# Expert 0's rows picked by one-hot matmuls from tiles kept on chip, index matmuls and overflow tables moved into the experts

## The chip, the cores and the metric

The kernel runs on one core of one Trainium2 chip. The metric is the device time of one execution in microseconds, as the median of several runs. The engines are TensorE (PE; its weight loads are listed as PEld), VectorE (DVE), ScalarE (ACT), GpSimd (POOL) and SyncE (SP), and transfers run on 16 DMA engines.

## The reference, cut to what matters

```python
SEQ = 512; D_MODEL = 1024; DEPTH = 2; N_EXPERTS = 16; N_GROUPS = 4; TOP_K = 2; D_EXPERT = 512

for l in range(DEPTH):
    sh1, sc1, g1, sh2, sc2, g2 = jnp.split(silu(c) @ w_ada[l] + b_ada[l], 6, axis=-1)
    h = modulate(rmsnorm(x, norm1_g[l]), sh1, sc1)
    x = x + g1 * mixer(h, ...)                  # retention, pooling, projections
    h = modulate(rmsnorm(x, norm2_g[l]), sh2, sc2)
    x = x + g2 * moe(h, ...)                    # the part that the change touches
return rmsnorm(x, final_g)

def moe(h, ...):
    probs = softmax(h @ w_router + b_router)    # 512 tokens x 16 experts
    # the group (of 4) with the largest sum of its two best, and in it the two best experts
    expert_idx, weights = route(h, ...)
    # every expert works on the tokens that chose it
    y_e = (silu(x_e @ w_gate[e]) * (x_e @ w_up[e])) @ w_down[e]
    # each token gets the weighted sum of its two experts' rows
```

All arrays are float32.

## The kernel before, in words

The program is written out by hand for each engine: every engine has its own function in which its instructions stand in order, and semaphores order the engines among each other (`wait_ge` waits, `then_inc` counts up). No planner moves anything. There are two layers, and each has a mixer of 17 groups of matmuls and then the experts.

*Weights.* All weights come as pieces of 512 KB through a ring of eight `raw` slots, which SyncE fills as `raw_used` counts up. In the expert stage eight more pieces per layer lie in `ahead`. Products are made at float32 accuracy from two parts: ScalarE writes the high part of a piece, `w_hi`, VectorE the rest, `w_lo = raw - w_hi`, both in rings of four slots, and TensorE makes three passes (`three_passes`, L1389 to L1392). An expert has 12 pieces (0 to 3 and 4 to 7 for gate and up, 8 to 11 for down), and each is six matmuls of 512 columns. `lo_e(n)` and `hi_e(n)` are numbered so that 12 to 15 in expert e are pieces 0 to 3 of expert e + 1; piece n needs the ring slot of piece n - 4 to be used.

*Second norm.* `norm_tile(l, 1, "h2", t)` normalises the four token tiles of 128 rows into `h_nat`, a buffer with two slots. From t = 2 on it waits for the transposes of tile t - 2 and for that tile's store to DRAM (`row_stored`). GpSimd stores each tile twice into `h_rows`. TensorE transposes the tiles for the router.

*Routing.* On VectorE `route_tokens` makes one-hot rows of both choices of each token (`hots`), whose sum is `chosen`. TensorE counts from it each token's place within its expert and each expert's total (`pos_ready`). VectorE copies the places into `pos`, picks each token's own into `posk` (`both_chosen`), and makes eight one-hot matrices `hot` (token against slot). TensorE multiplies them with the token numbers `hotid`; that gives for every expert the row number in each of its 128 slots, and VectorE converts these to `idx` and, with empty slots set to row 0, to `idx_any`. GpSimd then gathers the rows of experts 0 to 3 from `h_rows` into `xg0` to `xg3` with four indirect DMAs. TensorE transposes expert 0's rows (`gathered_transposes`), ScalarE and VectorE split them into `xgT_hi` and `xgT_lo`, and expert 0 starts. In between TensorE runs dummy matmuls of 512 columns (`keep_busy(n)`): 29 ahead of the counts, 11 behind them, 28 behind the index matmuls.

*Overflow.* An expert has 128 slots. If one had more tokens, extra blocks would run after expert 15. The tables for that are made in any case: the first part at the end of `route_tokens` (L1159 to L1188), the second in `overflow_slots` (L1190), which VectorE runs behind expert 0's `gathered_lo`, ahead of expert 0. Their results are read first at expert 15 (`slots_ready`).

*Expert stage.* In order on VectorE, `expert(l, e)` is: `lo_e(4)`, `lo_e(5)`, first half of the last expert's `y_out`, `hidden(0)`, `lo_e(6)`, second half of `y_out`, `lo_e(7)`, `hidT(0)`, `lo_e(8)`, `lo_e(9)`, `hidden(1)`, `lo_e(10)`, `hidT(1)`, `lo_e(11)`, `lo_e(12)`, the next expert's `gathered_lo` in two halves around `lo_e(13)`, `lo_e(14)`, `lo_e(15)`. TensorE runs pieces 0 to 5, the transposes of the hidden rows' first half, pieces 6 to 9 (the second half's transposes within piece 9), the next expert's `gathered_transposes`, and pieces 10 and 11. For each expert GpSimd gathers the rows of expert e + 4 and scatters `y_out` of expert e to `y_rows`.

Of the kernel before, what the change touches and what calls it, by code (L numbers as in the profile page):

```python
# [17 lines left out]
F32 = mybir.dt.float32  # L18
F32R = mybir.dt.float32r
I32 = mybir.dt.int32  # L20
# [4 lines left out]
P = 128  # L25
# [154 lines left out]
def build(nc, w, x_in, c_in, consts, rotary, ada_rows, pool_w, pool_scale, final_g, out):  # L180
# [7 lines left out]
    with ExitStack() as ctx:  # L188
# [11 lines left out]
        def sb(name, shape, dtype, offset):  # L200
            return nc.alloc_sbuf_tensor_at(name, shape, dtype, offset=offset)
# [52 lines left out]
        y_sq = sb("y_sq", [P, DV], F32, Dr + 10240)  # L254
        h_nat = sb("h_nat", [P, 2, D], F32, Dr)
        sig_ret = sb("sig_ret", [P, NT, 512], F32, Dr)

# [48 lines left out]
        chosen = router_small("chosen", 64, F32R)  # L306
        pos = router_small("pos", 64)
        ovn = router_small("ovn", 16)
# [9 lines left out]
        idx = small("idx", NE, I32)  # L318
        idx_any = small("idx_any", XG_SLOTS, I32)
        spare = small("spare", 1)  # L320
# [71 lines left out]
        chosen_ready = sem("chosen_ready")  # L392
        pos_ready = sem("pos_ready")
        hot_ready = sem("hot_ready")
        idx_sum = sem("idx_sum")
# [407 lines left out]
        def _(v):  # L803
# [69 lines left out]
            def norm_tile(l, which, name, t):  # L873

                if t == 0 and (l or which):
                    v.wait_ge(norm_rows, l * 64 + 32 * which)
                if t >= 2:
                    v.wait_ge(unit_ready, unit_value(l, name, 2 * (t - 2) + 1))
                    if which == 1:
                        v.wait_ge(row_stored[t % 2], l * 160 + 16)  # L880
                inverse_deviation(l * 8 + 4 * which, t)
                if which == 1 and t == NT - 1:

                    for half in range(2):
                        cols = slice(512 * half, 512 * half + 512)
                        v.scalar_tensor_tensor(h_nat[:, t % 2, cols], x[:, t, cols], x_rs[:, t:t + 1], scale_row[:, cols],
                                               ALU.mult, ALU.mult)
                        v.drain()
                        v.tensor_tensor(h_nat[:, t % 2, cols], h_nat[:, t % 2, cols], shift_row[:, cols],
                                        ALU.add).then_inc(h_ready if half else h_half, 1)  # L890
                    return
                v.scalar_tensor_tensor(h_nat[:, t % 2], x[:, t], x_rs[:, t:t + 1], scale_row[:], ALU.mult, ALU.mult)
                v.drain()
                v.tensor_tensor(h_nat[:, t % 2], h_nat[:, t % 2], shift_row[:], ALU.add).then_inc(h_ready, 1)

# [185 lines left out]
            def route_tokens(l):  # L1081
# [72 lines left out]
                v.wait_ge(idx_sum, l + 1)  # L1154
                v.tensor_scalar(idx_any[:], ps[:, 6, 64:64 + XG_SLOTS], -1.0, 0.0, ALU.add, ALU.max)
                v.tensor_scalar(idx[:], ps[:, 6, 64:80], -1.0, None, ALU.add).then_inc(idx_ready, 1)
                for q in range(2, W_SLOTS):
                    lo(l, MIX + q, RAW_MIX + q)
                v.tensor_scalar(ovn[:], ps[:, 7, 64:80], float(CAP), None, ALU.is_gt)  # L1159
                v.drain()  # L1160
                for level in range(2, LEVELS):
                    v.scalar_tensor_tensor(ovn[:], ps[:, 7, 64:80], float(level * CAP), ovn[:], ALU.is_gt, ALU.add)
                    v.drain()
# [24 lines left out]
                v.tensor_copy(ov_expert[:], ovt2[:, 0:NOV])  # L1188

            def overflow_slots(l):  # L1190
                rt3 = rt[:, 0:64].rearrange("p (t e) -> p t e", e=NE)
                pos3 = pos[:].rearrange("p (t e) -> p t e", e=NE)
# [3 lines left out]
                v.tensor_scalar(rt[:, 0:64], pos[:], float(CAP), None, ALU.is_ge)  # L1196
# [4 lines left out]
                both_chosen(slotf, pos[:])  # L1201
                v.memset(ov_base[:], float(NE * CAP))
                v.drain()
                v.sem_inc(slots_ready, 1)

# [7 lines left out]
            def expert(l, e):  # L1213
# [77 lines left out]
            for l in range(DEPTH):  # L1291
# [46 lines left out]
                with v.If(count > 0):  # L1338
                    v.wait_ge(w_used, l * PROD + (PROD + W_SLOTS))
                    apart(v)  # L1340
                    with v.Fori(0, count) as slot:
# [25 lines left out]
                        v.tensor_tensor(o_y[:, 512:1024], ps[:, 3], gate_row[:, 512:1024], ALU.mult).then_inc(ov_step, 1)  # L1367
                        v.drain()
                v.nop()
# [15 lines left out]
        def _(pe):  # L1385
# [89 lines left out]
            def norm_transposes(l, which, name, t):  # L1475
                if which == 0 or t < NT - 1:
                    pe.wait_ge(h_ready, l * 8 + (4 * which + t + 1))
                for j in range(2):
                    if which == 1 and t == NT - 1:
                        if j == 0:  # L1480
                            pe.wait_ge(h_half, l + 1)
                        else:
                            pe.wait_ge(h_ready, l * 8 + (4 + t + 1))
                    transposes(l, name, 2 * t + j, h_nat[:, t % 2, 512 * j:512 * j + 512])

# [72 lines left out]
            def misc(l, name):  # L1558
                if name == "u":
# [17 lines left out]
                    retention_pair(l, 2)  # L1577

            def gathered_transposes(l, e):

                pe.wait_ge(gathered[e % XG_SLOTS], 16 * ((l * NE + e) // XG_SLOTS + 1))
                for j in range(2):
                    for i in range(4):
                        c = (4 * j + i) * P
                        one = pe.transpose(ps[:, 4 + j, i * P:(i + 1) * P], xg[e % XG_SLOTS][:, c:c + P], ident)  # L1585
                    one.then_inc(xgT_ready, 1)

            def expert(l, e):
# [88 lines left out]
            for l in range(DEPTH):  # L1677
# [36 lines left out]
                for j in range(2):  # L1714
                    for t in range(NT):
                        one = pe.matmul(ps[:, 6, 64:80], hot[:, j, t], hotid[:, 64 * j + NE * t:64 * j + NE * t + NE],
                                        start=j == 0 and t == 0, stop=j == 1 and t == NT - 1)
                one.then_inc(idx_sum, 1)
# [46 lines left out]
        def _(pool):  # L1765
# [16 lines left out]
            def gather(l, e):  # L1782

                rows = idx_any[:, e:e + 1] if e < XG_SLOTS else idx[:, e:e + 1]
                pool.indirect_dma_start(xg[e % XG_SLOTS][:], None, h_rows, bass.IndirectOffsetOnAxis(ap=rows, axis=0),
                                        bounds_check=2 * T - 1, oob_is_err=False).then_inc(gathered[e % XG_SLOTS], 16)
# [11 lines left out]
            for l in range(DEPTH):  # L1798
# [32 lines left out]
                for t in range(NT):  # L1831
                    pool.wait_ge(h_ready, l * 8 + (4 + t + 1))
                    apart(pool)
                    pool.dma_start(h_tiles[t], h_nat[:, t % 2].unsqueeze(1).broadcast_to([P, 2, D])).then_inc(row_stored[t % 2], 16)
                pool.wait_ge(x_added, l * 8 + 8)
# [134 lines left out]
```

## Time and profile before

| | |
|---|---|
| median of 3 runs | 1544.78 us (1543.22 to 1546.78) |
| profiled execution, its own time | 1547.62 us |
| its span, first to last instruction | 1545.9 us |
| mean granted TensorE clock | 0.976 of full speed |
| busy share | TensorE 95%, VectorE 73%, ScalarE 50%, GpSimd 8% |
| DMA | 377 MB moved, 244 GB/s in the mean |

Times within the trace are microseconds from the start of the span. Layer 0's routing lies around 451 to 479, its experts from 479 to 770; layer 1's routing lies around 1196 to 1222, its experts up to 1513. A busy time is the sum of an engine's instructions in a stretch. Matmuls are pipelined, so a row of "11 matmuls, 2.77 us" counts from the start of the first to the end of the last, and their starts lie 0.23 us apart.

### The profile page before, as it was taken

How to read it: one execution, taken by the hardware profiler on the slowest of the kernel's cores; microseconds unless marked ns; L12 is line 12 of the kernel's file. 1: busy time of each engine (PE TensorE's matmuls, PEld its weight loads, DVE VectorE, ACT ScalarE, POOL GpSimd, SP SyncE). 2: the span in 40 equal slices, each digit the busy share in tenths (PEclk: the TensorE clock that was granted, in tenths of full speed). 3: DMA queues.
4: the chain of work that ended last, by engine and by line, in shares of the span. 5: the costliest groups of instructions: out<-in, count | busy, mean ns of one | idle time of the engine just before them, and what ended most of it. 6: DMA issues, size and time to landing. Idle time of an engine off the chain costs nothing.

```text
span 1545.9 us, 18774 instructions
## 1 busy us (share of the span) xinstructions
PE 1465.0 (95%) x6806; PEld 1169.4 (76%) x6806; DVE 1124.4 (73%) x1520; ACT 772.0 (50%) x1102; POOL 116.5 (8%) x141
## 2 busy tenths in 40 slices
PE   7999999999998999999959999999999999999991
PEld 2788878788877877787748888878887787788770
DVE  4684567555668999999977556754246799999995
ACT  2333433323344777777723334241234477777772
POOL 0000000000011111110000000000000111111100
PEclk8899999999999999999979999999999999999996
DMA  9556155455565999999875633632254879999984
GB/s 362 221 189 192 58 186 188 147 189 163 192 230 210 352 372 380 366 384 366 302 276 199 193 120 110 221 107 95 82 206 150 294 265 372 382 373 381 366 328 183
DMA packets 106705, 377.01 MB, mean 244 GB/s; under 512 B 16101, under 2 KB 16261, under 8 KB 105841
## 3 DMA queue, kind: packets, MB, share of 16 engines
q1 hardware_dynamic: 88512, 323.00, 58.2%
q0 software_dynamic: 15776, 44.36, 7.7%
q10 hardware_dynamic: 2322, 8.41, 1.4%
q8 instruction: 56, 0.92, 0.2%
q14 instruction: 39, 0.32, 0.1%
HBM read 358.45 MB, written 31.50 MB: 252 GB/s over the span
## 4 chain that ended last, share of the span: by engine, by line
PE 82%; DVE 9%; issue 3%; ACT 3%; DMA 1%; DVEq 1%; ACTq 0%; POOLq 0%
PE ps L1390 25%; PE ps L1392 23%; PE ps L1391 23%; DVE w_lo L1221 5%; ACT w_hi L688 2%; PE ps L1585 2%; PE ps L1472 2%; DVE y_out L1242 1%; PE ps L1652 1%; PE ps L1528 1%; PE ps L1532 1%; PE ps L1657 1%; DMA xg<-h_rows,idx_any 1%; PE ps L1573 1%; PE ps L1489 1%
## 5 line engine op out<-in xcount | busy, mean ns | idle before, releaser
L1221 DVE TENSOR_TENSOR w_lo<-raw,w_hi 128x1024 fp32r<-128x1024 f32 x360 | 426.4, 1219 | 14.0 <-ACT w_hi L688 13.6
L688 ACT ACTIVATE w_hi<-raw 128x1024 fp32r<-128x1024 f32 x360 | 367.6, 1056 | 27.9 <-PE ps L1392 27.7
L821 DVE TENSOR_TENSOR w_lo<-raw,w_hi 128x1024 fp32r<-128x1024 f32 x136 | 165.8, 1224 | 236.4 <-ACT w_hi L524 235.9
L524 ACT ACTIVATE w_hi<-raw 128x1024 fp32r<-128x1024 f32 x136 | 142.7, 1057 | 335.2 <-PE ps L1392 335.2
L1390 PE MATMUL ps<-w_hi,hT_lo 128*128 128x512 f32 x576 | 231.2, 401 | 2.9 <-DVE hT_lo L905 2.8
L1392 PE MATMUL ps<-w_hi,hT_hi 128*128 128x512 f32 x576 | 226.5, 393 | 0.0
L1391 PE MATMUL ps<-w_lo,hT_hi 128*128 128x512 f32 x576 | 226.4, 393 | 0.0
L1390 PE MATMUL ps<-w_hi,xgT_lo 128*128 128x512 f32 x512 | 206.2, 403 | 3.6 <-DVE xgT_lo L1210 1.2
L1392 PE MATMUL ps<-w_hi,xgT_hi 128*128 128x512 f32 x512 | 200.1, 391 | 0.0
L1391 PE MATMUL ps<-w_lo,xgT_hi 128*128 128x512 f32 x512 | 199.7, 390 | 0.0
L1390 PEld LDWEIGHTS ps<-w_hi,hT_lo 128*128 128x128 f32 x576 | 109.2, 190 | 29.2 <-DVE hT_lo L905 4.3
L1392 PEld LDWEIGHTS ps<-w_hi,hT_hi 128*128 128x128 f32 x576 | 109.3, 190 | 23.6
L1391 PEld LDWEIGHTS ps<-w_lo,hT_hi 128*128 128x128 f32 x576 | 109.4, 190 | 21.4
L1390 PEld LDWEIGHTS ps<-w_hi,xgT_lo 128*128 128x128 f32 x512 | 96.0, 187 | 35.6 <-DVE w_lo L1221 15.3
L833 DVE SCALAR_TENSOR_TENSOR ada_acc<-raw,cond,ada_acc 128x512 f32<-128x512 f32 x154 | 115.3, 749 | 7.5 <-issue 0.4
L1392 PEld LDWEIGHTS ps<-w_hi,xgT_hi 128*128 128x128 f32 x512 | 96.1, 188 | 20.9
L1391 PEld LDWEIGHTS ps<-w_lo,xgT_hi 128*128 128x128 f32 x512 | 96.2, 188 | 17.7
L1390 PE MATMUL ps<-w_hi,hidT_lo 128*128 128x512 f32 x256 | 108.2, 422 | 0.6 <-DVE hidT_lo L1233 0.6
L1390 PE MATMUL ps<-hT_hi,w_lo 128*128 128x512 f32 x256 | 105.1, 410 | 0.0
L1392 PE MATMUL ps<-w_hi,hidT_hi 128*128 128x512 f32 x256 | 100.4, 392 | 0.0
L1391 PE MATMUL ps<-w_lo,hidT_hi 128*128 128x512 f32 x256 | 100.1, 391 | 0.0
L1392 PE MATMUL ps<-hT_hi,w_hi 128*128 128x512 f32 x256 | 100.0, 391 | 0.0
(242 smaller groups left out, 2039.3 us busy)
## 6 DMA issues: line engine op xcount, KB each, us to landing
raw<-w SPq DMA_DIRECT2D x592, 512.0 KB, 5.7
h_rows<-h_nat POOLq DMA_DIRECT2D x8, 1024.0 KB, 6.8
ahead<-w SPq DMA_DIRECT2D x4, 2048.0 KB, 12.2
y_pair<-y_rows ACTq DMA_DIRECT2D x8, 1024.0 KB, 9.4
x_state<-x POOLq DMA_DIRECT2D x2, 2048.0 KB, 9.6
x<-x_state POOLq DMA_DIRECT2D x4, 1024.0 KB, 7.2
x<-x_in SPq DMA_DIRECT2D x4, 512.0 KB, 9.8
gate_row<-mod_rows POOLq DMA_DIRECT2D x4, 512.0 KB, 9.2
```

Source lines behind the costliest of these rows:

```text
L524: act.activation(w_hi[:, q % W_SLOTS], raw[:, r % RAW_SLOTS], ACT.Copy).then_inc(w_hi_ready, 1)
L688: act.activation(w_hi[:, n % W_SLOTS], expert_piece(e, n), ACT.Copy).then_inc(w_hi_ready, 1)
L821: v.tensor_tensor(w_lo[:, q % W_SLOTS], raw[:, r % RAW_SLOTS], w_hi[:, q % W_SLOTS], ALU.subtract).then_inc(raw_used, 1)
L833: one = v.scalar_tensor_tensor(ada_acc[:, acc], piece, c, ada_acc[:, acc], ALU.mult, ALU.add)
L1221: v.tensor_tensor(w_lo[:, n % W_SLOTS], expert_piece(e, n), w_hi[:, n % W_SLOTS], ALU.subtract).then_inc(raw_used, 1)
L1242: one = v.tensor_tensor(y_out[:, before % 2, cols], ps[:, 2 + half], gate_row[:, cols], ALU.mult)
L1390: pe.matmul(dst, a_lo, b_hi, start=start, stop=False)
L1391: pe.matmul(dst, a_hi, b_lo, start=False, stop=False)
L1392: return pe.matmul(dst, a_hi, b_hi, start=False, stop=stop)
L1472: one = pe.transpose(bank[:, i * P:(i + 1) * P], src[:, i * P:(i + 1) * P], ident)
L1489: pe.matmul(ps[:, 0], ones_r[:], ones_r[:].unsqueeze(1).broadcast_to([P, 4, P]), start=True, stop=True)
L1585: one = pe.transpose(ps[:, 4 + j, i * P:(i + 1) * P], xg[e % XG_SLOTS][:, c:c + P], ident)
```

## The change

- `h_nat` is left to the first norm. The second norm writes four tiles `h2[0]` to `h2[3]`, two in the place of `h_nat`, two in region `A`, and no longer waits for transposes or stores of earlier tiles. The stores to `h_rows` read from `h2`.
- Expert 0 is not gathered. VectorE makes four one-hot matrices `hot0` (float32) for expert 0 from `pos` and `chosen_f`, and TensorE selects expert 0's rows, already transposed, by `first_rows_selected`: 32 float32 matmuls, 8 column blocks times 4 tiles, straight into the PSUM banks in which the transposes stood.
- The index matmuls move into expert 0, behind its piece 1 (`row_ids`). `idx` follows on VectorE behind expert 0's `gathered_lo` and the first four `w_lo`. Experts 1 to 3 are gathered behind `idx` and behind the selection, as their slots overlap `h2`.
- The dummies become 9 behind the counts; the 28 are gone.
- `overflow_tables`, both parts of the overflow work in one, runs on VectorE at the end of `expert(l, 2)`. It reads the counts from `pos`, which is now 80 wide, and not from PSUM.
- `idx_any` is gone, and in the overflow loop VectorE waits for the block's scatter.

```diff
@@ norm_tile
-                if t >= 2:
+                if t >= 2 and which == 0:
                     v.wait_ge(unit_ready, unit_value(l, name, 2 * (t - 2) + 1))
-                    if which == 1:
-                        v.wait_ge(row_stored[t % 2], l * 160 + 16)
+                h = h2[t] if which else h_nat[:, t % 2]
@@ route_tokens
-                lo(l, MIX, RAW_MIX)
+                v.tensor_tensor(chosen_f[:], hots[:, 0:64], hots[:, 64:128], ALU.add)
                 v.wait_ge(pos_ready, l + 1)
-                v.tensor_copy(pos[:], ps[:, 7, 0:64])
-                v.drain()
-                both_chosen(posk, pos[:])
+                v.tensor_copy(pos[:], ps[:, 7, 0:80])
+                v.drain()
+                for t in range(NT):
+                    one = v.tensor_scalar(hot0[:, t], k("iota"), pos[:, NE * t:NE * t + 1], chosen_f[:, NE * t:NE * t + 1],
+                                          ALU.is_equal, ALU.mult)
+                one.then_inc(hot0_ready, 1)
+                both_chosen(posk, pos[:, 0:64])
                 for j in range(2):
                     for t in range(NT):
                         one = v.tensor_scalar(hot[:, j, t], k("iota"), posk[:, 4 * j + t:4 * j + t + 1], None, ALU.is_equal)
                 one.then_inc(hot_ready, 1)
-
+                lo(l, MIX, RAW_MIX)
+                gathered_lo(l * NE, 0, [0])
                 lo(l, MIX + 1, RAW_MIX + 1)
-                v.wait_ge(idx_sum, l + 1)
-                v.tensor_scalar(idx_any[:], ps[:, 6, 64:64 + XG_SLOTS], -1.0, 0.0, ALU.add, ALU.max)
-                v.tensor_scalar(idx[:], ps[:, 6, 64:80], -1.0, None, ALU.add).then_inc(idx_ready, 1)
+                gathered_lo(l * NE, 0, [1])
                 for q in range(2, W_SLOTS):
                     lo(l, MIX + q, RAW_MIX + q)
-                v.tensor_scalar(ovn[:], ps[:, 7, 64:80], float(CAP), None, ALU.is_gt)
+                v.wait_ge(idx_sum, l + 1)
+                v.tensor_scalar(idx[:], ps[:, 6, 496:512], -1.0, None, ALU.add).then_inc(idx_ready, 1)
+
+            def overflow_tables(l):
+
+                v.tensor_scalar(ovn[:], pos[:, 64:80], float(CAP), None, ALU.is_gt)
...
@@ expert, VectorE
+                if e == 2:
+                    overflow_tables(l)
@@ after route_tokens, VectorE
                 route_tokens(l)
-                gathered_lo(l * NE, 0)
-                overflow_slots(l)
@@ TensorE
+            def first_rows_selected(l):
+
+                pe.wait_ge(hot0_ready, l + 1)
+                for j in range(2):
+                    for i in range(4):
+                        c = (4 * j + i) * P
+                        for t in range(NT):
+                            one = pe.matmul(ps[:, 4 + j, i * P:(i + 1) * P], h2[t][:, c:c + P], hot0[:, t], start=t == 0,
+                                            stop=t == NT - 1)
+                    one.then_inc(xgT_ready, 1)
+
+            def row_ids(l):
+
+                pe.wait_ge(hot_ready, l + 1)
+                for j in range(2):
+                    for t in range(NT):
+                        one = pe.matmul(ps[:, 6, 496:512], hot[:, j, t], hotid[:, 64 * j + NE * t:64 * j + NE * t + NE],
+                                        start=j == 0 and t == 0, stop=j == 1 and t == NT - 1)
+                one.then_inc(idx_sum, 1)
@@ expert, TensorE
                 for n in range(6):
                     gate_up(n)
+                    if e == 0 and n == 1:
+                        row_ids(l)
@@ TensorE, routing
-                keep_busy(11)
-
-                pe.wait_ge(hot_ready, l + 1)
...
-                keep_busy(28)
-
+                keep_busy(9)
                 pe.wait_ge(acc_free, acc_value(l, NGROUP - 1, NT - 1))
-                gathered_transposes(l, 0)
+                first_rows_selected(l)
                 keep_busy(2)
@@ GpSimd
                 pool.wait_ge(idx_ready, l + 1)
+                pool.wait_ge(xgT_ready, l * NE * 2 + 4)
                 apart(pool)
-                for e in range(XG_SLOTS):
+                for e in range(1, XG_SLOTS):
                     gather(l, e)
```

## Rows read from the trace of the kernel before

**Rows 1.** The page's engine table: busy time, share of the span, instructions.
```profile
PE 1465.0 (95%) x6806; PEld 1169.4 (76%) x6806; DVE 1124.4 (73%) x1520; ACT 772.0 (50%) x1102; POOL 116.5 (8%) x141
```
**Rows 2.** Windows over expert 3 of layer 0: length, busy times, clock, DMA.
```profile
533.36:551.56 18.20, 18.12 (x85) 14.54 (x84) 17.61 (x21) 14.23 (x19) 2.38 (x2) 1.00 0.98 367
```
**Rows 3.** The chain of waits in expert 3: start, time on the chain.
```profile
538.76 0.24 PE ps L1392
...
539.30 1.06 ACT w_hi L688
...
542.21 1.15 DVE w_lo L1221
...
543.40 0.50 PE ps L1390
```
**Rows 4.** Timeline of VectorE in expert 3: start, time, instruction, idle before.
```profile
534.60 4.62 DVE L1221 TENSOR_TENSOR w_lo<-raw,w_hi 128x1024 fp32r<-128x1024 f32 x4
...
540.38 1.22 DVE L1221 TENSOR_TENSOR w_lo<-raw,w_hi 128x1024 fp32r<-128x1024 f32 x1 [0.23 <-ACT w_hi L688]
```
**Rows 5.** Timeline of VectorE, second norm and routing of layer 0.
```profile
442.17 0.16 DVE L870 RECIPROCAL x_rs<-x_std 128x1 f32<-128x1 f32 x1 [1.25 <-ACT x_std L544]
...
463.17 0.22 DVE L1145 COPY pos<-ps 128x64 f32<-128x64 f32 x1
...
464.19 1.66 DVE L1150 TENSOR_SCALAR hot<-const,posk 128x128 fp32r<-128x128 f32 x8
...
467.08 0.17 DVE L1156 TENSOR_SCALAR idx<-ps 128x16 int32<-128x16 f32 x1
...
469.45 0.16 DVE L1159 TENSOR_SCALAR ovn<-ps 128x16 f32<-128x16 f32 x1
...
474.12 0.17 DVE L1188 CAST ov_expert<-ovt 128x7 int32<-128x7 f32 x1
...
479.27 0.30 DVE L1193 TENSOR_SCALAR ovd<-ovd 128x16 f32<-128x16 f32 x1
...
482.08 2.36 DVE L1221 TENSOR_TENSOR w_lo<-raw,w_hi 128x1024 fp32r<-128x1024 f32 x2 [0.19 <-issue]
```
**Rows 6.** Timeline of TensorE, routing of layer 0.
```profile
462.25 2.77 PE L1489 MATMUL ps<-ones_r 128*128 128x512 f32 x11
465.91 1.06 PE L1716 MATMUL ps<-hotid,hot 128*128 128x16 f32 x8 [0.89 <-DVE hot L1150]
...
476.77 1.06 PE L1585 MATMUL ps<-const,xg 128*128 128x128 f32 x8 [3.34 <-DMA xg<-h_rows,idx_any]
...
478.91 0.47 PE L1390 MATMUL ps<-w_hi,xgT_lo 128*128 128x512 f32 x1 [0.60 <-DVE xgT_lo L1210]
```
**Rows 7.** Timeline of TensorE, routing of layer 1.
```profile
1206.77 2.75 PE L1489 MATMUL ps<-ones_r 128*128 128x512 f32 x11
...
1221.93 0.47 PE L1390 MATMUL ps<-w_hi,xgT_lo 128*128 128x512 f32 x1 [0.60 <-DVE xgT_lo L1210]
```
**Rows 8.** Timeline of GpSimd, first gather of layer 0; landing times of all gathers.
```profile
468.27 1.07 POOL L1785 DMA_INDIRECT xg<-h_rows,idx_any  x1 [13.97 <-issue]
...
DMA to landing us min/median/max: 4.2/8.3/9.4
```
**Rows 9.** Timeline of TensorE, retention scores of layer 0 (float32 matmuls).
```profile
163.72 1.95 PE L1511 MATMUL ps<-qT,kT 128*128 128x128 f32 x16
165.50 0.38 PE L1517 MATMUL ps<-y,k_rot 128*128 128x256 f32 x1
```
**Rows 10.** Windows in which TensorE stood still or the clock was lower.
```profile
473.43:476.77 3.34, 0.01 (x1) 0.03 (x1) 0.71 (x3) 0.00 (x0) 0.00 (x0) 1.00 1.00 402
770.14:775.25 5.11, 0.00 (x1) 0.00 (x0) 5.07 (x6) 1.70 (x2) 1.19 (x1) 1.00 0.09 34
775.25:790.77 15.52, 1.95 (x9) 1.57 (x9) 9.78 (x10) 3.42 (x6) 0.00 (x0) 0.50 0.79 311
790.77:795.60 4.83, 4.83 (x11) 3.81 (x12) 3.96 (x5) 0.55 (x3) 0.00 (x0) 0.50 0.97 362
1212.30:1215.60 3.30, 3.30 (x9) 2.55 (x9) 2.96 (x9) 0.00 (x0) 2.08 (x2) 0.50 0.76 220
```

More of the change, by code:

```diff
@@ L255, in build @@
         h_nat = sb("h_nat", [P, 2, D], F32, Dr)
+        h2 = [sb(f"h2_{t}", [P, D], F32, o) for t, o in enumerate((Dr, Dr + 4096, A, A + 4096))]
+        hot0 = sb("hot0", [P, NT, P], F32, A + 28672)
         sig_ret = sb("sig_ret", [P, NT, 512], F32, Dr)
@@ L306, in build @@
         chosen = router_small("chosen", 64, F32R)
-        pos = router_small("pos", 64)
+        chosen_f = router_small("chosen_f", 64)
+        pos = router_small("pos", 80)
         ovn = router_small("ovn", 16)
@@ L318, in build @@
         idx = small("idx", NE, I32)
-        idx_any = small("idx_any", XG_SLOTS, I32)
         spare = small("spare", 1)
@@ L393, in build @@
         pos_ready = sem("pos_ready")
+        hot0_ready = sem("hot0_ready")
         hot_ready = sem("hot_ready")
@@ L885, in norm_tile @@
                         cols = slice(512 * half, 512 * half + 512)
-                        v.scalar_tensor_tensor(h_nat[:, t % 2, cols], x[:, t, cols], x_rs[:, t:t + 1], scale_row[:, cols],
+                        v.scalar_tensor_tensor(h[:, cols], x[:, t, cols], x_rs[:, t:t + 1], scale_row[:, cols],
                                                ALU.mult, ALU.mult)
                         v.drain()
-                        v.tensor_tensor(h_nat[:, t % 2, cols], h_nat[:, t % 2, cols], shift_row[:, cols],
-                                        ALU.add).then_inc(h_ready if half else h_half, 1)
+                        v.tensor_tensor(h[:, cols], h[:, cols], shift_row[:, cols], ALU.add).then_inc(h_ready if half else h_half, 1)
                     return
-                v.scalar_tensor_tensor(h_nat[:, t % 2], x[:, t], x_rs[:, t:t + 1], scale_row[:], ALU.mult, ALU.mult)
+                v.scalar_tensor_tensor(h[:, 0:D], x[:, t], x_rs[:, t:t + 1], scale_row[:], ALU.mult, ALU.mult)
                 v.drain()
-                v.tensor_tensor(h_nat[:, t % 2], h_nat[:, t % 2], shift_row[:], ALU.add).then_inc(h_ready, 1)
+                v.tensor_tensor(h[:, 0:D], h[:, 0:D], shift_row[:], ALU.add).then_inc(h_ready, 1)
             def norm_lo(l, name, t):
@@ L1188, in route_tokens @@
                 v.tensor_copy(ov_expert[:], ovt2[:, 0:NOV])
-            def overflow_slots(l):
                 rt3 = rt[:, 0:64].rearrange("p (t e) -> p t e", e=NE)
-                pos3 = pos[:].rearrange("p (t e) -> p t e", e=NE)
+                pos3 = pos[:, 0:64].rearrange("p (t e) -> p t e", e=NE)
                 v.tensor_scalar(ovd[:, 16:32], ovd[:, 16:32], float(NE - 1), float(CAP), ALU.add, ALU.mult)
@@ L1195, in overflow_slots @@
                 tt(ovd[:, 16:32], ovd[:, 16:32], k("ecap"), ALU.subtract)
-                v.tensor_scalar(rt[:, 0:64], pos[:], float(CAP), None, ALU.is_ge)
+                v.tensor_scalar(rt[:, 0:64], pos[:, 0:64], float(CAP), None, ALU.is_ge)
                 v.drain()
@@ L1200, in overflow_slots @@
                 tt(pos3, rt3, pos3, ALU.add)
-                both_chosen(slotf, pos[:])
+                both_chosen(slotf, pos[:, 0:64])
                 v.memset(ov_base[:], float(NE * CAP))
-                v.drain()
-                v.sem_inc(slots_ready, 1)
+                v.drain().then_inc(slots_ready, 1)
             def gathered_lo(E, slot, halves=(0, 1)):
@@ L1367, in _ @@
                         v.tensor_tensor(o_y[:, 512:1024], ps[:, 3], gate_row[:, 512:1024], ALU.mult).then_inc(ov_step, 1)
-                        v.drain()
+                        v.wait_ge(ov_y, b * 16 + 16)
                 v.nop()
@@ L1483, in norm_transposes @@
                             pe.wait_ge(h_ready, l * 8 + (4 + t + 1))
-                    transposes(l, name, 2 * t + j, h_nat[:, t % 2, 512 * j:512 * j + 512])
+                    h = h2[t] if which else h_nat[:, t % 2]
+                    transposes(l, name, 2 * t + j, h[:, 512 * j:512 * j + 512])
             def keep_busy(n):
@@ L1577, in misc @@
                     retention_pair(l, 2)
+            def first_rows_selected(l):
[14 more added lines that the diff above has]
+                one.then_inc(idx_sum, 1)
             def gathered_transposes(l, e):
-                pe.wait_ge(gathered[e % XG_SLOTS], 16 * ((l * NE + e) // XG_SLOTS + 1))
+                turn = l * 3 + e // XG_SLOTS if e % XG_SLOTS == 0 else (l * NE + e) // XG_SLOTS + 1
+                pe.wait_ge(gathered[e % XG_SLOTS], 16 * turn)
                 for j in range(2):
@@ L1710, in _ @@
                 one.then_inc(pos_ready, 1)
-                keep_busy(11)
-                pe.wait_ge(hot_ready, l + 1)
[L1714 to L1718, printed above, removed]
-                keep_busy(28)
+                keep_busy(9)
                 pe.wait_ge(acc_free, acc_value(l, NGROUP - 1, NT - 1))
-                gathered_transposes(l, 0)
+                first_rows_selected(l)
                 keep_busy(2)
@@ L1782, in gather @@
             def gather(l, e):
-                rows = idx_any[:, e:e + 1] if e < XG_SLOTS else idx[:, e:e + 1]
-                pool.indirect_dma_start(xg[e % XG_SLOTS][:], None, h_rows, bass.IndirectOffsetOnAxis(ap=rows, axis=0),
+                pool.indirect_dma_start(xg[e % XG_SLOTS][:], None, h_rows, bass.IndirectOffsetOnAxis(ap=idx[:, e:e + 1], axis=0),
                                         bounds_check=2 * T - 1, oob_is_err=False).then_inc(gathered[e % XG_SLOTS], 16)
@@ L1833, in _ @@
                     apart(pool)
-                    pool.dma_start(h_tiles[t], h_nat[:, t % 2].unsqueeze(1).broadcast_to([P, 2, D])).then_inc(row_stored[t % 2], 16)
+                    pool.dma_start(h_tiles[t], h2[t][:].unsqueeze(1).broadcast_to([P, 2, D])).then_inc(row_stored[t % 2], 16)
                 pool.wait_ge(x_added, l * 8 + 8)
```

2 lines of the change are left out of this document (1 added, 1 removed).

## The prediction, as it was recorded before the change ran

> **What bounds the kernel now.** I read the page's engine table first, then the windows over one expert, the chain of waits inside an expert, VectorE's timeline there, and last the timelines of VectorE, TensorE and GpSimd between router and expert 0. The page says TensorE is busy 95% of the span and VectorE 73% [rows 1]. That mean hides what matters here. In the expert stage, one expert takes 18.20 us, of which TensorE is busy 18.12 and VectorE 17.61 [rows 2]. VectorE has 0.59 us to spare per expert. The chain of waits shows the two engines coupled: piece 3's matmul, the gate's activation and `w_hi` on ScalarE, `w_lo` of piece 6 on VectorE, a `y_out` half, `w_lo` of piece 7, then TensorE's piece 7 [rows 3]. VectorE's only idle time before that `w_lo` is 0.23 us [rows 4]. So in an expert a microsecond added to VectorE is paid for; in the routing stretch it is hidden, because TensorE fills time with dummy matmuls and waits for gathered rows [rows 5, 6].
>
> The routing stretch of layer 0 runs from the counts (VectorE copies `pos` at 463.17) to expert 0's first matmul at 478.91 [rows 5, 6]. In layer 1 the last of these is at 1221.93 [rows 7].
>
> **The change, part by part.**
>
> *Selection instead of a gather: a gain.* Before, expert 0 waits for posk, eight one-hots, an index matmul, `idx`, GpSimd's start (468.27) and the gather's landing; TensorE starts the transposes at 476.77 and the expert 2.14 us later [rows 5, 6, 8]. After, four one-hots suffice. The counts end near 462.4, for the dummies behind them start at 462.25 [rows 6], so the copy of `pos` can start about 462.5; the copy and its drain take 0.29 (463.17 to the next instruction), four one-hots at the pace of the eight `hot` rows, 1.66 in all, about 0.9, so they stand at 463.7 [rows 5]. TensorE is then still in its dummies: eleven took 2.77 us, a matmul each 0.2275, so nine end their issue near 464.4 in layer 0 and 1208.9 in layer 1 [rows 6, 7]. The second scalar operand of `hot0` is a form that the trace does not show; the 0.7 us left before 464.4 cover it, from nothing to nearly double the price.
>
> Then come 32 real float32 matmuls of 128x128 on 128 columns. The nearest row is the retention scores: 16 records for 8 source matmuls, started at 163.72, next work at 165.50, so 0.2225 us a matmul [rows 9]. 32 of them are 7.1 us. Bounds: the transposes of the same size, one record each (8 in 1.06), would make it 3.6, and half clock 14.2; I take 7.1, since operands and type are those of the scores. The two dummies behind cost 0.46; the first half's hi and lo parts are ready by then (2.14 us from first transpose to expert before). Expert 0 starts at 464.4 + 7.1 + 0.5 = 472.0, 6.9 us earlier; in layer 1 at 1216.5, 5.4 earlier.
>
> *Index matmuls moved into expert 0, behind piece 1.* Eight records; in the trace the work behind them starts 0.9 us after them [rows 6]. They lie in TensorE's own order, so 0.9 us per layer is paid. VectorE now waits for `idx_sum` with expert 0's `lo_e(4)` queued behind it: idx at 475.9, `lo_e(4)` done near 477.0, needed by TensorE at 478.3. (Piece 1 ends at 472.0 + 2 x 1.365 = 474.7, the index matmuls at 475.6, pieces 2 and 3 at 478.3; a piece is six matmuls of 0.2275.) No stall.
>
> *The gathers of experts 1 to 3* now start behind `idx` and `xgT_ready`. GpSimd began 1.2 us after `idx` (467.08 to 468.27) and the landings take 4.2 to 9.4 us, 8.3 in the middle [rows 5, 8]: expert 1's rows land near 485.4, and TensorE reaches their transposes at 475.6 + eight pieces of 1.365 + 0.9 of hidden transposes = 487.4. Cover 2.0 us. Later gathers have an expert's time more.
>
> *Four `h2` tiles, no waits for `row_stored` and units.* Before the third tile's reciprocal VectorE waits for ScalarE's deviation, 1.25 us, and not for a store [rows 5]. So nothing is gained. The stores themselves stay where they are. The move of `w_lo` for piece 0 behind the one-hots is covered: 1.2 us, done at 467, needed at 472.
>
> *Overflow tables moved into expert 2: a loss.* Before, the first part ran from 469.45 to 474.29 while rows were being gathered, the second from 479.27 to 482.08, ahead of `lo_e(4)` but with pieces 0 to 3 staged [rows 5]. Both were free: counted back by two periods from expert 3's start at 533.36, expert 1 started at 496.96, so expert 0 took 18.05 us, no more than the others [rows 2, 6]. Together they are 4.84 + 2.81 = 7.65 us; reading `pos` from SBUF may take a tenth or two off, so 7.5 to 7.65, I take 7.6. Now they stand at the end of `expert(2)` behind `lo_e(15)`, ahead of expert 3's `lo_e(4)`, `lo_e(5)`, `y_out`, `hid`, `lo_e(6)` and `lo_e(7)`. In the trace of before expert 3 starts at 533.36, and the four `w_lo` at 534.60 are its pieces 2, 3 (numbered 14, 15), 4 and 5, 1.13 apart, so `lo_e(4)` starts at 536.87 and TensorE has pieces until 533.36 + 4 x 1.365 = 538.8 [rows 2, 4]. `lo_e(4)` would now end at 545.6: TensorE idles 6.8 us. What the coupled chain forgives is the 0.23 us before `lo_e(6)` [rows 4]; from `lo_e(7)` on TensorE is 7.4 us late, and nothing behind gives it back, since every expert runs on the same 18.20 us cycle. Bounds: 7.65 (nothing forgiven) and 5.5 (all 2.0 us of staged work forgiven). I take 7.4 per layer.
>
> *TensorE's clock.* TensorE idles like that once in the trace: with no matmul from 770.14 the granted clock was 1.00 over 5.11 us and 0.50 after it, so at half, 1.2 of 2.4 GHz. When work came back, 4.83 us and 11 matmuls passed at half clock [rows 10]. At full clock eleven take 2.5, so 2.3 is lost. A second fall, with matmuls running, lasted 3.30 us [rows 10], which loses 1.65. Behind the tables TensorE would also wait 0.65 us for `lo_e(6)` and `lo_e(7)`, which hides that much: 1.0 to 1.65 is paid. I take 1.5 per layer; if the clock holds, 0.
>
> The Trainium skill, "TensorE: Matmul & The Clock Gate", section "HAM oscillation", says that an idle gap between bursts of matmuls drops the clock to half, and that this is paid again at each gap. By that rule the tables' stall costs more than its own length; the trace agrees in the one gap it has.
>
> **The sum** against the profiled execution's own 1547.62 us: - 6.9 - 5.4 + 2 x 0.9 = - 10.5 for the routing; + 2 x 7.4 = + 14.8 for the tables; + 2 x 1.5 = + 3.0 for the clock. Net + 7.3. The profiled execution stands 2.84 above the median of the runs, 1544.78; the difference carried over gives 1552.1.
>
> **Rivals.**
> 1. *Tables exposed, clock holds* or falls just once: + 4.3 to + 5.8, so 1549.1 to 1550.6. For it: in layer 0's routing the clock held 1.00 across 3.34 us without matmuls [rows 10]. Against: 6.8 us of idleness are longer than the 5.11 after which it fell.
> 2. *The tables are hidden* (faster): VectorE's 7.6 us fit beside TensorE's staged work. All the routing gain stays if they cost nothing, 1534.3; the sign turns where they cost under 5.2 us per layer, clock included, 1544.8. For it: a ring of four slots stands between the engines, and 2.0 us of pieces are staged where the tables begin [rows 2, 4]. Against: VectorE is idle for only 0.59 us per expert [rows 2], and to get from 7.6 under 5.2 the staged pieces must be forgiven in full and the clock must hold too.
> 3. *Gathers late for expert 1*: landing at 9.4 instead of 8.3 is still inside the cover; beyond 2.0 us each microsecond counts, and TensorE idles in a second place. With 3 us over in each layer, 1558. Against: one gather fewer runs ahead of it.
> 4. *The selection gives little*: were the clock at half in the 32 matmuls, 7.1 would be lost in each layer and 1566 result; that needs the stretch before them to look idle. In layer 1 the clock did fall after the small count and index matmuls. In one layer for a part of the time it could cost 2.
>
> **Chances.** Forecast 0.50, rival 1 0.25, rival 2 0.13, rival 3 0.06, rival 4 0.06. The forecast's own range, from the bounds of stall and clock, is 1549.5 to 1555. The range that holds 8 in 10 takes in rival 1 and the near parts of 2 and 4: 1546 to 1556.5. A measurement of this kernel can tell about 0.2%, 3.1 us, from no change. Faster by more: rival 2 without its upper end, 0.12. Within: the ends of rivals 1 and 2, 0.12. Slower: 0.76.
>
> **What the profile after would show.** Right: `hot0` done about 1 us after `pos`; 64 records of 0.11 us; expert 0's first matmul near 472.0 and 1216.5; the index matmuls behind piece 1; no wait on a gather; about forty small VectorE instructions behind `lo_e(15)` of expert 2; TensorE idle near 6.8 us after piece 3 of expert 3, half clock behind it; 18.2 us between `y_rows` stores elsewhere, 25.6 to 27 there. Wrong if the gap between those stores grows by under 5 us, if TensorE waits on `xg`, or if the 32 matmuls take far from 7.1 us.

## The result, and the profile after

The changed kernel takes 1551.43 us (median of 20 runs, 1547.69 to 1554.84), the kernel before 1545.69 us beside it (20 runs, 1543.22 to 1552.10). The ratio is 1.0034, 95% interval 1.0025 to 1.0044: 5.3 us slower at the ratio, against a forecast of + 7.3. The time itself was forecast at 1552.1. In the profiled executions the change took 1554.23 us with a span of 1552.5, that of before 1547.62 with a span of 1545.9, so the traces differ by 6.6 us.

The page's engine table hides the loss as it hid the limit. Against [rows 1] TensorE has 52 records more and 0.4 us more of busy time, VectorE 1.6 us more. The span grew by 6.6 all the same.

```profile
PE 1465.4 (94%) x6858; PEld 1173.3 (76%) x6858; DVE 1126.0 (73%) x1528; ACT 772.0 (50%) x1102; POOL 115.2 (7%) x139
```

**The gain, in the routing stretch.** VectorE's timeline there, which answers to [rows 5] (start, time, instruction, idle before):

```profile
461.16 0.23 DVE L1132 TENSOR_TENSOR chosen<-hots 128x64 fp32r<-128x64 f32 x1
...
462.53 0.24 DVE L1146 COPY pos<-ps 128x80 f32<-128x80 f32 x1 [0.18 <-PE ps L1739]
462.85 1.11 DVE L1149 TENSOR_SCALAR hot<-const,pos,chosen_f 128x128 f32<-128x128 f32 x4
...
468.92 0.69 DVE L1216 TENSOR_TENSOR xgT_lo<-ps,xgT_hi 128x512 fp32r<-128x512 f32 x1 [1.33 <-ACT xgT_hi L724]
...
475.89 0.17 DVE L1164 TENSOR_SCALAR idx<-ps 128x16 int32<-128x16 f32 x1 [0.44 <-PE ps L1602]
```

And TensorE's, which answers to [rows 6, 7], in layer 0 and then in layer 1:

```profile
462.35 2.33 PE L1496 MATMUL ps<-ones_r 128*128 128x512 f32 x9
464.52 7.30 PE L1593 MATMUL ps<-hot,h 128*128 128x128 f32 x64
471.58 0.71 PE L1496 MATMUL ps<-ones_r 128*128 128x512 f32 x2
472.13 0.40 PE L1396 MATMUL ps<-w_hi,xgT_lo 128*128 128x512 f32 x1
...
474.90 0.95 PE L1602 MATMUL ps<-hotid,hot 128*128 128x16 f32 x8
475.71 0.49 PE L1396 MATMUL ps<-w_hi,xgT_lo 128*128 128x512 f32 x1
...
1212.06 7.30 PE L1593 MATMUL ps<-hot,h 128*128 128x128 f32 x64
...
1219.66 0.40 PE L1396 MATMUL ps<-w_hi,xgT_lo 128*128 128x512 f32 x1
```

The four one-hots (VectorE, line 1149) are done at 463.96, while TensorE still has its nine dummies. The 32 selection matmuls are 64 records from 464.52 to the dummies at 471.58, 7.06 us. No engine waits between them, and expert 0 starts at 472.13. The index matmuls take 0.81 us of TensorE's order. GpSimd gathers from 477.08, and TensorE transposes expert 1's rows at 487.45 without a wait:

```profile
477.08 1.07 POOL L1805 DMA_INDIRECT xg<-h_rows,idx  x1 [22.66 <-issue]
...
DMA to landing us min/median/max: 7.1/7.7/9.3
```

**The loss, in expert 3.** VectorE's timeline around the tables. They run from 530.98 to the next `w_lo` at 538.42, 7.44 us:

```profile
530.98 0.16 DVE L1168 TENSOR_SCALAR ovn<-pos 128x16 f32<-128x16 f32 x1
...
537.50 0.29 DVE L1079 TENSOR_REDUCE slotf<-rt 128x8 f32<-128x128 f32 x1
537.89 0.06 DVE L1209 MEMSET ov_base<- 128x1 f32 x1
538.42 2.36 DVE L1227 TENSOR_TENSOR w_lo<-raw,w_hi 128x1024 fp32r<-128x1024 f32 x2 [0.47 <-issue]
```

TensorE's timeline in the same place: its pieces run out, and the next one waits 6.59 us for that `w_lo`.

```profile
532.72 0.39 PE L1398 MATMUL ps<-w_hi,xgT_hi 128*128 128x512 f32 x1
539.70 0.79 PE L1396 MATMUL ps<-w_hi,xgT_lo 128*128 128x512 f32 x1 [6.59 <-DVE w_lo L1227]
540.29 0.63 PE L1397 MATMUL ps<-w_lo,xgT_hi 128*128 128x512 f32 x1
```

The waits view has it as one row for both layers (total, times, longest):

```profile
PE ps L1396 <- DVE w_lo L1227: 13.1, 2, 6.6
```

The windows (columns as in [rows 2]: TensorE, its weight loads, VectorE, ScalarE, GpSimd, granted clock, DMA share, GB/s) show what the idleness did to the clock:

```profile
532.95:536.80 3.85, 0.16 (x1) 0.00 (x0) 2.92 (x16) 2.27 (x3) 0.00 (x0) 1.00 0.63 256
536.80:537.80 1.00, 0.00 (x0) 0.00 (x0) 0.80 (x3) 0.00 (x0) 0.00 (x0) 0.52 0.02 8
539.70:543.30 3.60, 3.60 (x9) 2.83 (x10) 3.60 (x5) 0.00 (x0) 0.00 (x0) 0.50 0.65 193
543.30:544.00 0.70, 0.70 (x4) 0.57 (x3) 0.70 (x2) 0.00 (x0) 0.00 (x0) 0.73 0.80 322
```

Read the first row for VectorE: 16 instructions, busy 2.92 of 3.85 us, with a `drain` of the program between one small result and the next. The tables are a chain of latencies, not a volume of work. The second row is the fall to 1.2 GHz. Then nine matmuls run at half clock, and it is back at full speed near 543.6. The tables are 29 instructions on VectorE; the prediction had about forty.

**Term by term.** The stretch from `chosen` (VectorE) to the first `y_rows` store (GpSimd) holds the routing and most of expert 0 and excludes whatever went before. Every later store marks an expert, 18.20 apart in the steady state, so the tables and the clock are what the two gaps around expert 3 hold above 36.4. The lines for layer 0, first the two of before, then those after:

```profile
461.06 0.23 DVE L1131 TENSOR_TENSOR chosen<-hots 128x64 fp32r<-128x64 f32 x1
...
506.61 1.21 POOL L1794 DMA_INDIRECT y_rows<-y_out,idx  x1 [27.02 <-DVE y_out L1242]
```
```profile
500.75 1.21 POOL L1814 DMA_INDIRECT y_rows<-y_out,idx  x1 [18.52 <-DVE y_out L1248]
...
518.94 1.20 POOL L1814 DMA_INDIRECT y_rows<-y_out,idx  x1 [15.51 <-DVE y_out L1248]
...
544.24 1.21 POOL L1814 DMA_INDIRECT y_rows<-y_out,idx  x1 [22.62 <-DVE y_out L1248]
...
563.83 1.20 POOL L1814 DMA_INDIRECT y_rows<-y_out,idx  x1 [17.06 <-DVE y_out L1248]
```

| | layer 0 before | after | change | forecast | layer 1 change | forecast |
|---|---|---|---|---|---|---|
| `chosen` to first store | 45.55 | 39.59 | - 5.96 | - 6.0 | - 4.48 | - 4.5 |
| the two gaps above 36.4 | 0 | 8.49 | + 8.49 | + 8.9 | + 8.50 | + 8.9 |

(Layer 1: 44.08 before, 39.60 after; gaps 25.27 and 19.63. Layer 0: 25.30 and 19.59.) The four sum to + 6.55, the difference of the spans is 6.6. That the rest of the program took the same in both traces is chance: over the nine traces of this document, layer 0's `chosen` starts anywhere from 457.00 to 462.59. The stretches above are therefore firmer than the difference of two spans.

### The profile page after: what moved, and what is told of

Same layout as the page of the kernel before. It is cut to its first block, busy times and chain, and to the rows that moved or that the text cites. A ratio compares the mean times of both kernels' runs of the same rounds, so it can differ in the third digit from the quotient of the medians.

```text
span 1552.5 us, 18878 instructions
## 1 busy us (share of the span) xinstructions
PE 1465.4 (94%) x6858; PEld 1173.3 (76%) x6858; DVE 1126.0 (73%) x1528; ACT 772.0 (50%) x1102; POOL 115.2 (7%) x139
## 4 chain that ended last, share of the span: by engine, by line
PE 82%; DVE 10%; issue 3%; ACT 3%; DVEq 1%; DMA 1%; ACTq 0%
PE ps L1396 24%; PE ps L1398 23%; PE ps L1397 23%; DVE w_lo L1227 5%; ACT w_hi L691 2%; PE ps L1478 2%; PE ps L1613 2%; PE ps L1682 1%; DVE y_out L1248 1%; PE ps L1593 1%; PE ps L1535 1%; PE ps L1539 1%; PE ps L1580 1%; PE ps L1687 1%; PE ps L1660 1%
## 5 line engine op out<-in xcount | busy, mean ns | idle before, releaser
L1397 PEld LDWEIGHTS ps<-w_lo,xgT_hi 128*128 128x128 f32 x512 | 97.1, 190 | 18.3
```

Of the source, the lines that this page charges most:

```text
L1397: pe.matmul(dst, a_hi, b_lo, start=False, stop=False)
```

## The experiments

A time of an experiment is the median of its timed runs, and its ratio is to the kernel before on the same chip (1545.66 us beside the first four, 1546.97 beside the last three).

**The tables left out.** It leaves out the overflow tables: the number of overflow blocks and the other results that the tables would give are set to zero once, at the start. Nothing else of the change is touched.

```diff
                 if e == 2:
-                    overflow_tables(l)
+                    v.sem_inc(slots_ready, 1)
```

> The changed kernel without the overflow tables: only the count of extra blocks is set to zero once, which is what the tables give for these inputs. Theory (VectorE's 7.3 us of tables are paid in full, plus a fall of TensorE's clock behind them): what is left is the routing gain, about -10.4 us against the kernel before, ratio 0.9933, 15.7 us below the changed kernel; the gap between the y_rows stores of experts 1 and 2 falls from 25.3 to 18.2 us. Rival (the tables are hidden beside staged pieces, the loss comes from elsewhere, such as the later gathers or the selection): the ratio stays near 1.003.

Measured: 1536.44 us (6 runs), ratio 0.9926 (0.9911 to 0.9942), 11.4 us faster than before. `chosen` to first store is 39.60 in layer 0, as after the change, and the stores stand 18.2 apart (502.19, 520.38, 538.60, 556.83). So the selection part alone is a gain of about its forecast size (10.5), and all that the change loses hangs on the tables.

**The tables alone.** The other half: the kernel before, still gathering expert 0's rows, with both parts of its overflow work put where the change has them.

```diff
@@ route_tokens
-        pos = router_small("pos", 64)
+        pos = router_small("pos", 80)
...
+            def overflow_tables(l):
...
@@ expert
+                if e == 2:
+                    overflow_tables(l)
@@ the stage
-                overflow_slots(l)
```

> The kernel before with one part of the change: both parts of the overflow work moved to the end of expert 2, nothing else. Theory: + 2 x (7.4 + 1.1 to 1.5) = +17 to +18 us, ratio 1.0113, with TensorE idle about 6.6 us behind piece 3 of expert 3 and half clock for about 4 us after. Rival (the move is cheap and the selection is what costs): under +5 us, ratio under 1.003.

Measured: 1563.77 us (5 runs), ratio 1.0118 (1.0101 to 1.0136), 18.2 us slower. TensorE's timeline and window there:

```profile
540.29 0.80 PE L1391 MATMUL ps<-w_hi,xgT_lo 128*128 128x512 f32 x1 [6.26 <-DVE w_lo L1221]
```
```profile
540.29:545.20 4.91, 4.91 (x12) 3.85 (x13) 4.88 (x6) 0.00 (x0) 0.37 (x1) 0.50 0.72 219
```

The price is 9.0 in layer 0 by the stores (gaps 24.99 and 20.43) and 9.1 in layer 1 (25.31 and 20.16), some 0.5 more than with the selection. The stalls are not longer (6.26 and 6.60), but the clock was at half for 5.8 us after work came back in layer 0 (until 546.1) and 5.2 in layer 1, instead of 3.9. The two halves, - 11.4 and + 18.2, sum to 6.8, which is the whole change within what the intervals allow. In the old routing stretch little came back: from `chosen` to the first store it took 43.90 in layer 1, where the kernel before took 44.08, which agrees with the prediction that they were free there. In layer 0 it took 44.22, 1.33 less than before. There the first gather landed 7.0 us after its start instead of 8.4; whether the missing tables had a part in that is not shown.

**The clock alone.** The change, with 26 dummy matmuls behind piece 3 of expert 3. They fill the idleness, so the stall stays and the clock doesn't fall.

```diff
+                    if e == 3 and n == 3:
+                        for _ in range(26):
+                            pe.matmul(ps[:, 7], ones_r[:], ones_r[:]..., start=True, stop=True)
```

> The changed kernel with 26 dummy matmuls of 512 columns (5.9 us) on TensorE behind piece 3 of expert 3, into a bank that nobody reads there: the stall is filled, its length stays. Theory (the clock's fall costs 1.1 to 1.5 us per layer of its own): granted clock 1.00 through the stall, 2 to 3 us below the changed kernel, ratio 1.0015 to 1.0020. Rival (VectorE bounds those pieces anyway, the clock costs nothing): ratio 1.0034 as with the changed kernel, the pieces behind waiting on w_lo.

Measured: 1548.53 us (12 runs), ratio 1.0021 (1.0006 to 1.0035). That interval overlaps the change's (1.0025 to 1.0044), so the timed runs alone don't prove the difference; the trace does.

```profile
528.84 6.06 PE L1669 MATMUL ps<-ones_r 128*128 128x512 f32 x26
535.58 0.50 PE L1396 MATMUL ps<-w_hi,xgT_lo 128*128 128x512 f32 x1 [0.69 <-DVE w_lo L1227]
```
```profile
528.91:535.58 6.67, 5.98 (x27) 4.63 (x25) 5.05 (x21) 2.28 (x3) 0.00 (x0) 1.00 0.35 142
535.58:539.60 4.02, 4.02 (x18) 3.13 (x18) 4.02 (x6) 0.73 (x2) 0.00 (x0) 1.00 0.69 191
```

The clock is 1.00 throughout, TensorE is "busy" all along, and the two gaps around expert 3 are 25.31 and 18.23: 7.14 above the rhythm, and 7.10 in layer 1 (25.28 and 18.22). So the 8.49 and 8.50 of the change are 7.14 and 7.10 of stall and 1.35 and 1.40 of clock. A TensorE that is kept busy is not a TensorE that gets its data.

**Four parts.** The 27 steps of the tables in four parts, behind experts 2 to 5.

```diff
                 if e == 2:
-                    overflow_tables(l)
+                    tables.extend(table_steps(l))
+                if 2 <= e <= 5:
+                    for _ in range(-(-len(tables) // (6 - e))):
+                        table_step()
```

> The changed kernel with the same table instructions in four parts of about 1.8 us, behind experts 2, 3, 4 and 5. Theory (the coupled chain forgives 0.23 us per expert, the clock holds across stalls of 1 us): 4 x 1.6 = 6.3 us per layer, so -10.4 + 12.6 = +2.2, ratio 1.0014, and each of four y_rows gaps is 19.8 us instead of 18.2. Rival (what TensorE has staged beyond VectorE's next w_lo, 0.85 us, is forgiven each time): -10.4 + 2 x 3.8 = -2.8, ratio 0.998. Rival (all 2 us of staged pieces are forgiven): the parts are free, ratio 0.9933.

Measured: 1547.70 us (12 runs), ratio 1.0011 (0.9999 to 1.0023). The four gaps are 19.68, 19.78, 19.92 and 19.73, together 6.3 above four times 18.20. On VectorE the parts took 1.80, 1.90, 2.05 and 1.83 us, together 7.6, so about 0.32 us of each was forgiven, the little that each expert's cycle has. The clock doesn't fall (1.00 from 531 to 540); TensorE waits about a microsecond each time:

```profile
532.61 0.50 PE L1413 MATMUL ps<-w_hi,xgT_lo 128*128 128x512 f32 x1 [0.96 <-DVE w_lo L1241]
```

This shows that in this cycle the ring of staged pieces gives next to no credit. A part of 1.90 us, shorter than the 2.0 us of pieces that were staged, still costs 1.58. Both rivals fell here: with 0.85 us forgiven each time a gap would have been about 19.2.

**One step at a time.** The same 27 steps, each put where VectorE is about to wait for ScalarE anyway: ahead of `lo_e(6)`, ahead of `lo_e(10)` and behind it, from expert 2 on.

```diff
                 hidden(0)
+                table_step()
                 lo_e(6)
...
                 hidden(1)
+                table_step()
                 lo_e(10)
+                table_step()
                 hidT(1)
...
-                if e == 2:
-                    overflow_tables(l)
+                if e == 1:
+                    tables.extend(table_steps(l))
```

> The changed kernel with the 27 steps of the tables issued one at a time (about 0.27 us each) where VectorE waits anyway in an expert: ahead of lo_e(6), lo_e(10) and the second hidT, from expert 2 on, nine experts long. Theory (VectorE's idle 0.23, 0.18 and 0.17 us of an expert take them in, only some 0.05 us per expert ahead of lo_e(6) is paid): within 1 us per layer of the kernel without tables, -10 us against the kernel before, ratio 0.993 to 0.994, y_rows gaps at most 18.3 us. Rival (every microsecond of VectorE in an expert is paid, as the sum of the prediction has it for the block): 2 x 7.3 us more than without tables, ratio 1.002.

Measured: 1535.18 us (6 runs), ratio 0.9934 (0.9916 to 0.9951), by the intervals as fast as with no tables at all, and faster than both kernels. VectorE's timeline in expert 2, and the window over that expert, to be laid beside [rows 2, 4]:

```profile
517.83 0.41 DVE L1247 TENSOR_TENSOR hid<-tmp,ps 128x256 f32<-128x256 f32 x1
518.16 0.17 DVE L1187 SCALAR_TENSOR_TENSOR ovn<-pos,ovn 128x16 f32<-128x16 f32 x1
518.42 1.23 DVE L1241 TENSOR_TENSOR w_lo<-raw,w_hi 128x1024 fp32r<-128x1024 f32 x1
```
```profile
514.98:533.19 18.21, 18.13 (x86) 14.54 (x84) 17.90 (x26) 14.22 (x19) 2.37 (x2) 1.00 1.01 380
```

VectorE is busy for 17.90 us where it was 17.61, and the expert still takes 18.2. The step stands in the 0.23 us of idleness that [rows 4] have in front of that `w_lo`. The first stores are 18.2 apart (496.78, 514.98, 533.19, 551.39, 569.59). Later three gaps are wider (18.39, 18.28 and 18.30), one of them above the 18.3 that was expected; the steps there are on 64 to 128 columns and take 0.22 to 0.28 us instead of 0.17. In all the steps cost about 0.4 us per layer by the stores, where the undivided block cost 8.5.

**The ids late.** The kernel with the spread steps, with the index matmuls behind piece 4 of expert 0 instead of piece 1, and `idx` on VectorE moved back to just ahead of `hidden(0)`, to measure the cover of the gather, which the forecast had at 2.0 us.

```diff
-                v.wait_ge(idx_sum, l + 1)
-                v.tensor_scalar(idx[:], ps[:, 6, 496:512], -1.0, None, ALU.add).then_inc(idx_ready, 1)
...
+                if e == 0:
+                    v.wait_ge(idx_sum, l + 1)
+                    v.tensor_scalar(idx[:], ps[:, 6, 496:512], -1.0, None, ALU.add).then_inc(idx_ready, 1)
                 hidden(0)
...
-                    if e == 0 and n == 1:
+                    if e == 0 and n == 4:
                         row_ids(l)
```

> The kernel e5_spread with the index matmuls, and idx behind them, 3 pieces (4.1 us) later in expert 0, which starts the gathers of experts 1 to 3 by as much later. Theory (the gather for expert 1 had a cover of 1 to 3 us in the changed kernel): TensorE waits 1 to 3 us for xg in each layer's expert 0, +2 to +6 us against e5_spread, ratio 0.995 to 0.998. Rival (the cover is larger than 4.1 us): no wait on xg, the time of e5_spread.

Measured: 1536.80 us (6 runs), ratio 0.9941 (0.9923 to 0.9960). The gather starts at 479.37, and the transposes of expert 1's rows still don't wait:

```profile
479.37 1.40 POOL L1823 DMA_INDIRECT xg<-h_rows,idx  x1 [26.74 <-DVE idx L1270]
```
```profile
485.70 1.04 PE L1631 MATMUL ps<-const,xg 128*128 128x128 f32 x8
```

That is 6.33 us from the gather's start to the use of its rows, and in layer 1 6.37 (1217.76 to 1224.13). So no wait came of a start 4.1 us later, and the expected wait of 1 to 3 us was wrong. In the changed kernel's own trace the first gather landed 7.1 us after its start, 3.3 us before its use (477.08 to 487.45), and here it was in time within 6.3. First landings differ from trace to trace (8.4 in that of before, 7.0 with the tables alone) at DMA shares of 0.99 in both; why was not settled.

**The tables first.** The change with the tables behind `idx`, ahead of expert 0's `lo_e(4)`, the place where the kernel before had the second part.

```diff
                 route_tokens(l)
+                overflow_tables(l)
...
-                if e == 2:
-                    overflow_tables(l)
```

> The changed kernel with the tables behind idx, ahead of expert 0, where the kernel before had its second part, and not in expert 2. Theory (the new routing has no stretch left that hides a block; expert 0 forgives 1.4 us instead of 0.2, as VectorE idles there longer): 6.0 us and 1.1 us for the clock per layer, -10.4 + 14.2 = +3.8, ratio 1.0025. Rival (it is the place inside the expert stage that costs, at expert 0 the block would be hidden as before): ratio 0.993.

Measured: 1549.95 us (12 runs), ratio 1.0029 (1.0014 to 1.0045).

```profile
484.38 0.79 PE L1395 MATMUL ps<-w_hi,xgT_lo 128*128 128x512 f32 x1 [5.83 <-DVE w_lo L1227]
```
```profile
484.38:488.40 4.02, 4.02 (x10) 3.15 (x11) 3.69 (x4) 0.00 (x0) 0.00 (x0) 0.50 0.75 251
```

From `chosen` to the first store it takes 47.76 us in layer 0 and 47.05 in layer 1, where the change without tables takes 39.60: 8.2 and 7.45, where expert 2 has 8.5. So it isn't the third expert that makes them dear. Once expert 0 starts early, the wait for the gather in which they were free [rows 5, 6] is gone, and the block is paid here too. The ratio came out as expected, the price per layer above the 7.1 of the theory. The clock can account for that: at half it ran for 4.5 us after work came back in layer 0 and 2.9 in layer 1. If half of that is lost, 2.2 and 1.5 (an estimate), 5.9 and 6.0 are left for the stall, the 6.0 that was expected. No run with dummies tests it.

## Why the prediction was right

*The selection.* Forecast - 6.9 and - 5.4, with 0.9 back for the index matmuls. It rested on three readings: one-hots ready before the dummies end (463.96, while the nine dummies give way to the selection at 464.52), 0.2225 us for a float32 matmul of that shape as in the retention scores [rows 9] (0.2206 measured), and a clock of 1.00 through the stretch. All held, and expert 0 started at 472.13 where 472.0 was forecast. In layer 1 it started at 1219.66, forecast 1216.5; `chosen` stood 3.11 us later in that trace (1208.69 against 1205.58), so it is the same gain. The layer's net stands at - 5.96 and - 4.48, and without the tables the whole kernel gains 11.4. The two-operand one-hots were dearer than assumed, 1.11 us for four instead of 0.9, and the margin took it. Rivals 3 and 4 fell with this: no wait on `xg`, no half clock in the 32 matmuls.

*The tables.* Forecast 7.6 us of VectorE, 6.8 of TensorE idle, 7.4 paid. Measured 7.44 and 7.39 (layers 0 and 1), 6.59 and 6.55, and 7.14 and 7.10. The mechanism was that of the prediction: `lo_e(4)` late, staged pieces used up, nothing behind it that gives time back. Four parts show it most sharply, since a part that the ring should have absorbed was not absorbed. What was forgiven, 0.30 us of the block and 0.32 of each part, is close to the 0.23 us that VectorE idles ahead of `lo_e(6)` [rows 4], and it is there that the single steps went in for nearly nothing. That this short wait, and not the 0.59 us of idleness in the whole cycle [rows 2], sets the limit is argued from these figures; no run changes the wait itself. It isn't so everywhere: before the change the second part stood ahead of expert 0's `lo_e(4)`, with pieces 0 to 3 staged, and was free [rows 5], and with the tables first some 1.4 us of 7.3 was forgiven by the estimate above. Rival 2, the hidden tables, needed under 5.2 per layer; 8.5 was paid.

*The clock.* Forecast 1.5 per layer, 1.35 measured by the dummies. It fell 3.7 us into the idleness and came back 3.9 us after work did. Rival 1, in which it holds, fell: the traces show 0.50 in both layers, and the gaps with the clock kept up are smaller by 1.35 and 1.40. Its argument against itself, that 6.8 us are longer than 5.11, named one case; with the tables first the clock fell after 2.0 us without matmuls in layer 1 (see the last section). The Trainium skill, "TensorE: Matmul & The Clock Gate", section "HAM oscillation — how this bites in real kernels", says that a burst of matmuls behind an idle gap starts at half clock and pays for it anew at each gap. The trace agrees at the stalls of 6.59 and 6.55 us, one in each layer; at the 0.96 us of the four parts the clock held.

*The size of the whole.* Working with one trace against its own span, the forecast was + 7.3 and the traces gave + 6.6. The 0.7 between them are the stall at 7.4 instead of 7.14 and the clock at 1.5 instead of 1.35, in two layers. The timed runs say + 5.3 (4 to 7 by the interval). That the traces say 6.6 lies within the scatter of single executions: after's profiled one, 1554.23, stands 2.8 above its median, that of before 1.9 above its own. That 1551.43 comes so near to 1552.1 is in part luck. The change was smaller than forecast by 2.0, and the kernel before took 0.9 more beside it than in the three runs that the forecast started from.

*What the prediction had wrong* without effect on the time is the cover of the gather: 2.0 us forecast, 3.3 in the changed kernel's trace, and a start 4.1 us later still cost nothing. By that reckoning the index matmuls had to stand early in expert 0; they need not. It also had the growth of the store gaps at expert 3 alone (25.6 to 27). The first gap is 25.30, and the rest of the price is in the next one, 19.59.

## What to carry to other kernels

Work that was free in a wait must be given a new place when the wait is removed; price the change with and without it, for here a part worth - 11.4 us was sold with one that cost + 17. Small dependent steps are cheap one at a time in an engine's own short waits (27 steps, about 0.4 us) and dear in a row (8.5 us with the clock). In this stage, where two engines both run above 96%, the ring between them paid for next to nothing of a stall: look for idle time in the cycle, not for staged pieces.

## What the runs showed of the hardware

The granted clock held through 3.34 us without matmuls [rows 10], and in the trace of before it fell 5.11 us after the last one. In the stalls behind the tables it fell at no fixed point: after 3.7 us in both layers of the change, after 5.3 and 5.0 with the tables alone, and after 3.6 and 2.0 with the tables first. What agrees is the stretch at half clock, 6.7 to 6.8 us from fall to return in all six. Four of them, each over 6.60 us of it (the change and the tables alone, both in layer 0; the tables first, layers 0 and 1):

```profile
536.90:543.50 6.60, 3.80 (x9) 3.03 (x10) 5.88 (x11) 0.00 (x0) 0.00 (x0) 0.50 0.38 114
539.40:546.00 6.60, 5.71 (x15) 4.45 (x15) 5.77 (x7) 0.00 (x0) 1.17 (x1) 0.50 0.62 193
482.20:488.80 6.60, 4.42 (x10) 3.47 (x11) 5.50 (x8) 0.00 (x0) 0.00 (x0) 0.50 0.67 223
1226.30:1232.90 6.60, 2.86 (x7) 2.28 (x8) 5.85 (x13) 0.26 (x1) 0.99 (x1) 0.50 0.62 186
```

So the later the clock falls within a stall, the more of the slow stretch lies behind it and is paid: 2.9 us where it fell after 2.0, 5.8 where it fell after 5.3. That difference, 4.5 against 2.9 us at half clock, can also account for the 0.7 us between the two layers with the tables first. What sets the moment of the fall no run here shows. Other falls in these kernels lasted 3.30 us and over 20 [rows 10].

An indirect gather whose landings had a median of 8.3 us in one kernel was in time for use 6.3 us after its start in another. A float32 matmul of 128x128 on 128 columns took 0.2206 us, 32 in a row. A one-hot of 128x128 with two operands from memory cost 0.28 us, with one 0.21 before and 0.23 in the changed kernel; the two also write different types, so the second operand's share isn't isolated.
